# Another order of maps and projection units in the second mixer of a two-block transformer kernel

## What is computed

```python
def token_mixer(h, w_in, w_out, lq1, lk1, lq2, lk2, subln_gain, rel_bias, layer):
    proj = h @ w_in
    ...
    oa = diff_attention(qa, ka, va, lam, rel_bias[:, :2 * N_DIFF_HEADS])
    oa = rmsnorm(oa, subln_gain) * (1.0 - lam0)
    ...
    ob = dilated_attention(qb, kb, vb, rel_bias[:, 2 * N_DIFF_HEADS:])
    ...
    mixed = jnp.concatenate([oa, ob], axis=-1)
    return mixed @ w_out
```

## Time and profile before

| | before |
|---|---|
| runs | 1048.93, 1046.16, 1045.85 us |
| the profiled execution's own time | 1050.62 us |
| its span | 1048.5 us |
| PE busy | 1006.0 us (96%) |
| DVE, ACT, POOL busy | 666.6, 477.8, 80.7 us |
| moved by DMA | 175.77 MB, 168 GB/s over the span |

### The profile page before, as it was taken

How to read it: one execution, slowest core, us unless ns; L and a number is a source line. 1 busy time by engine, 2 the same in 40 slices (tenths; PEclk the granted TensorE clock), 3 DMA queues, 4 the chain that set the end, 5 groups by cost and what they waited for, 6 DMA issues and landing times. The chain is left out here.

```text
span 1048.5 us, 17492 instructions
## 1 busy us (share of the span) xinstructions
PE 1006.0 (96%) x7506; PEld 958.7 (91%) x7506; DVE 666.6 (64%) x848; ACT 477.8 (46%) x573; POOL 80.7 (8%) x202
## 2 busy tenths in 40 slices
PE   4999998999999999999999999999997899999996
PEld 4999998989999999999899999989997899999995
DVE  3578865685876866666675555556667366555554
ACT  4455555554435544444543434444434254434343
POOL 0010104532140000000000000000002000000001
PEclk9999999999999999999999999999999699999999
DMA  8656545342456555464556565654333146565641
GB/s 280 203 162 190 179 155 162 125 157 96 146 165 223 189 189 202 166 209 166 182 170 199 179 199 178 200 163 161 121 121 121 47 162 215 164 201 177 197 146 40
DMA packets 143558, 175.77 MB, mean 168 GB/s; under 512 B 4661, under 2 KB 130777, under 8 KB 143482
## 3 DMA queue, kind: packets, MB, share of 16 engines
q1 hardware_dynamic: 138794, 168.30, 49.4%
q10 hardware_dynamic: 4688, 6.36, 1.9%
HBM read 173.58 MB, written 4.22 MB: 170 GB/s over the span
## 5 line engine op out<-in xcount | busy, mean ns | idle before, releaser
L336 PE MATMUL ps<-hTh,wh 128*128 128x256 f32 x1512 | 431.3, 285 | 7.5 <-DVE wl L1227 6.9
L1227 DVE TENSOR_TENSOR wl<-raw,wh 128x2048 fp32r<-128x2048 f32 (+1 forms) x156 | 356.6, 2287 | 115.2 <-ACT wh L841 114.9
L336 PE MATMUL ps<-hTl,wh 128*128 128x256 f32 x1512 | 428.2, 283 | 0.0
L336 PE MATMUL ps<-hTh,wl 128*128 128x256 f32 x1512 | 428.1, 283 | 0.0
L841 ACT ACTIVATE wh<-raw 128x2048 fp32r<-128x2048 f32 (+1 forms) x158 | 299.5, 1900 | 177.9 <-PE ps L336 177.4
L336 PEld LDWEIGHTS ps<-hTh,wh 128*128 128x128 f32 x1512 | 289.7, 192 | 11.1 <-DVE wl L1227 6.7
L336 PEld LDWEIGHTS ps<-hTl,wh 128*128 128x128 f32 x1512 | 289.7, 192 | 1.4
L336 PEld LDWEIGHTS ps<-hTh,wl 128*128 128x128 f32 x1512 | 289.6, 192 | 0.2
L336 PE MATMUL ps<-wh,yTh 128*128 128x512 f32 (+1 forms) x328 | 123.9, 378 | 1.4 <-DVE BIGT L1625 1.3
L336 PE MATMUL ps<-wl,yTh 128*128 128x512 f32 (+1 forms) x328 | 124.5, 380 | 0.0
L336 PE MATMUL ps<-wh,yTl 128*128 128x512 f32 (+1 forms) x328 | 122.6, 374 | 0.0
(11 more groups left out here) (253 smaller groups left out, 811.6 us busy)
## 6 DMA issues: line engine op xcount, KB each, us to landing
raw<-in_ffn_w_up SPq DMA_DIRECT2D x44, 1024.0 KB, 5.3
raw<-in_w_in SPq DMA_DIRECT2D x40, 1024.0 KB, 5.3
raw<-in_ffn_w_down SPq DMA_DIRECT2D x33, 1024.0 KB, 5.1
raw<-in_ffn_w_gate SPq DMA_DIRECT2D x22, 1024.0 KB, 5.3
raw<-in_w_out SPq DMA_DIRECT2D x8, 1024.0 KB, 5.0
raw<-in_mem_kv_w SPq DMA_DIRECT2D x4, 1024.0 KB, 5.0
scr_f<-scr_r ACTq DMA_DIRECT2D x1, 3072.0 KB, 15.3
raw<-in_w_br_hgrn SPq DMA_DIRECT2D x2, 1024.0 KB, 5.0
```

The source lines that it names most:

```text
L336: ins = pe.matmul(o, l(k), r(k), start=first and k == ks[0] and j == 0, stop=last and k == ks[-1] and j == 2)
L1227: dve.tensor_tensor(wl[j % NS][:, 0:n], raw[j % NR][:, 0:n], wh[j % NS][:, 0:n].bitcast(F32), ALU.subtract).then_inc(w_lo, 1)
```

## The change

Seven things are altered, all between these two points.

- The maps are in another order: the eight diff maps first, then the eight dil maps. The weights are in the order qa0, ka0, va0, qa1, ka1, va1, qb0, kb0, qb1, kb1, vb0, vb1.
- `rows_out` and `toks_out` take a function `mid` that is called between their halves, so PE's map steps stand one at each half unit, where two stood at the end of a unit.
- Six buffers hold turned maps, PT0, PT1 and four in `Hn` (idle in this stage), so a dil map's values may come up to six maps after its turns. The values of maps 8 to 15 are issued in groups of two and three, behind vb's units.
- `scores` of map 8 and 12 also wait for qb; `diff_out` waits for the head before it.
- ACT and DVE have their work in a new order, with `exps` 14 and 15 and the drain of vb1 behind the split of OA.
- The output projection's first two units run side by side in four banks: the k blocks 0 to 3 of both (OA), then 4 and 5 (OB's first half), then 6 and 7, with the last steps of the maps and the two turns of OB between them.
- `project`'s stretches for the first block are tuples in place of functions, with the same waits.

```diff
+        PT2 = PT + [Hn[:, 512 * j:512 * j + 512] for j in range(4)]
...
+        def turned(a, i):
+            return PT[i % 2] if a == 0 else PT2[i % 6]
...
-            def rows_out(key, banks):
+            def rows_out(key, banks, mid=None):
...
+                    if m == 0 and mid:
+                        mid()
...
+            def step(s=None, t=None, vs=()):
+                if s is not None:
+                    scores(1, s)
+                if t is not None:
+                    turns(1, t)
+                for v in vs:
+                    values(1, v)
+
             toks_out(("va", 0), W)
...
+            step(0)
+            rows_out(("qa", 1), W, mid=lambda: step(1, 0))
+            step(2, 1, [0])
+            rows_out(("ka", 1), W, mid=lambda: step(3, 2, [1]))
+            step(None, 3, [2])
+            toks_out(("va", 1), W, mid=lambda: step(4, None, [3]))
+            step(5, 4)
+            rows_out(("qb", 0), W, mid=lambda: step(6, 5, [4]))
+            step(7, 6, [5])
+            rows_out(("kb", 0), W, mid=lambda: step(None, 7, [6]))
+            step(None, None, [7])
+            rows_out(("qb", 1), W, mid=lambda: step(8))
+            step(9, 8)
+            rows_out(("kb", 1), W, mid=lambda: step(10, 9))
+            step(11, 10)
+            toks_out(("vb", 0), W, mid=lambda: step(12, 11))
+            step(13, 12)
             pe.wait_ge(oa_done, 1)
             for p in range(2):
                 turn(("oa", p), OA, p, 512)
...
+            toks_out(("vb", 1), W, mid=lambda: step(14, 13, [8, 9]))
+            step(15, 14, [10, 11])
...
+            ts_a = begin_unit(key_a, W)
+            pe.wait_ge(*free(("oa", 0)))
+            pe.wait_ge(*free(("oa", 1)))
+            stretch(key_a, ts_a, (0, 1, 2, 3))
+            step(None, 15, [12, 13, 14])
+            ts_b = begin_unit(key_b, T)
+            stretch(key_b, ts_b, (0, 1, 2, 3))
+            pe.wait_ge(*free(("bo", 0)))
+            turn(("ob", 0), OB, 0, 512)
+            step(None, None, [15])
+            pe.wait_ge(*free(("ob", 0)))
+            stretch(key_a, ts_a, (4, 5))
+            pe.wait_ge(*free(("bo", 1)))
+            turn(("ob", 1), OB, 1, 512)
+            stretch(key_b, ts_b, (4, 5))
+            pe.wait_ge(*free(("ob", 1)))
+            stretch(key_a, ts_a, (6, 7))
+            stretch(key_b, ts_b, (6, 7))
+            toks_out(("wo", 4, PIECES[2]), W, yhT_at)
```

More of the change, by code:

```diff
@@ L25 @@
 MAPS1 = [("fox", h) for h in range(8)] + [("mem", h) for h in range(4)]
-MAPS2 = ([("diff", h, j) for h in (0, 1) for j in (0, 1)] + [("dil", h) for h in range(4)]
-         + [("diff", h, j) for h in (2, 3) for j in (0, 1)] + [("dil", h) for h in range(4, 8)])
-OBANK = {("diff", 0): 6, ("diff", 1): 7, ("dil", 0): 6, ("diff", 2): 7, ("diff", 3): 6, ("dil", 1): 7}
+MAPS2 = [("diff", h, j) for h in range(4) for j in (0, 1)] + [("dil", h) for h in range(8)]
+OBANK = {("diff", 0): 6, ("diff", 1): 7, ("diff", 2): 6, ("diff", 3): 7, ("dil", 0): 6, ("dil", 1): 7}
 class Banks:
@@ L613, in attend @@
             def attend(a, i):
[L614 to L618, removed]
+                if 0 <= i - 1 < 12:
                     turns(a, i - 1)
-                if 0 <= i - 2 < n:
+                if 0 <= i - 2 < 12:
                     values(a, i - 2)
-                if not early and i < n:
+                if i < 12:
                     scores(a, i)
@@ L709, in project @@
                         weights(i)
-                        for ks, before in stretches:
-                            before()
+                        for ks, operands_made in stretches:
+                            pe.wait_ge(*operands_made)
                             for m in range(2):
@@ L1607, in attend @@
             def attend(a, i):
-                n = 12 if a == 0 else 16
-                early = a == 1 and i != 12
-                if early and i < n:
-                    guards(a, i)
-                if 0 <= i - 1 < n:
+                if 0 <= i - 1 < 12:
                     copies(a, i - 1)
-                if 0 <= i - 2 < n:
+                if 0 <= i - 2 < 12:
                     outs(a, i - 2)
-                if not early and i < n:
+                if i < 12:
                     guards(a, i)
@@ L1708, in project @@
                     begin(key)
[L1709 to L1713 removed]
+                    if n == 0 or (k, n) == (4, 1):
                         for m in range(2):
@@ L1831, in dve_program @@
                 turn_lo_part(("oa", p), yTh, yTl, p, gs)
-            attend(1, 16)
+            guards(1, 14)
+            copies(1, 13)
+            begin(("vb", 1))
+            guards(1, 15)
+            copies(1, 14)
+            outs(1, 11)
+            copies(1, 15)
+            turn_lo_part(("ob", 0), hTh, hTl, 0)
+            outs(1, 15)
+            turn_lo_part(("ob", 1), hTh, hTl, 1)
             project(4)
```

194 lines of the change are left out of this document (89 added, 105 removed).

## The result

| | before | after |
|---|---|---|
| median of the runs | 1046.16 us (3 runs, known when the prediction was made) | 1034.20 us (4 runs, 1034.12 to 1034.22) |
| the kernel before, run beside it | 1047.55 us (4 runs, 1045.85 to 1049.07) | |
| ratio after / before | | 0.9873 [0.9853, 0.9893] |
| the profiled execution's own time, its span | 1050.62, 1048.5 us | 1034.2, 1032.1 us |
| PE, DVE, ACT, POOL busy | 1006.0, 666.6, 477.8, 80.7 us | 997.5, 666.4, 478.3, 80.6 us |

The kernel is 1.3% faster. Against the base of the prediction, 1046.16, that is 12.0 us. DVE, ACT and POOL do the same work. PE's busy time fell by 8.5 us although it has the same matmuls; a matmul that runs at the low clock counts as busy for longer.

A forecast was written before the change was run, and what follows sets the result against it. PE was taken to bound the kernel, 104.0 us of the 122.1 us stretch being work. New waits and seams made 107.0, 15.1 less; 1046.2 - 15.1 = 1031.1 us, range 1028.0 to 1037.

The forecast's parts named there:

- likeliest case: Whole kernel: the forecast as summed, 1031.1 us, own range 1028.5 to 1033, chance 0.66.
- the clock rival: Stretch: clock falls all the same, or unprofiled runs never had so much to win; 1033.6 to 1037 us, chance 0.18.
- 18.1 us of waits and clock: va0 to first turn behind third output unit: 122.1 us less 104.0 of work; about 12 waits, some 6 clock.
- Map steps, slack 1.9 us: Steps at half units: 4.57 us from scores to turns where 2.69 are needed; pairs' waits, 2.0 us, go.
- The knot at 794: PE's waits for bank, copy and exponentials near 794 us, some 3.5 us, go with six buffers and later dil values.
- OA's norm covered by 1.5 us: OA scaled on POOL at 791.4 us, turned by PE at 792.9, so the old 2.2 us wait goes.
- The rival of the other order: At OA's norm DVE's weight split takes the port before POOL's product: PE waits 1.4 us, 1032.2 us total, chance 0.10.
- Entry wait 1.4: Entry into the output projection: PE waits 1.4 us for ACT's drain of vb1, now behind the last map's exponentials.
- OB 1.1 and 0.2: OB's turns: 1.1 us of wait stay open at the first half, 0.2 at the second; old 1.7 and 0.8 go.
- No fall of the clock: Stretch: new waits of 1.4 and 1.1 us, some 10 us apart, bring no low clock; 6 us come back.
- New stretch 107.0: va0 to first turn behind third output unit: 104.0 + 1.4 + 1.1 + 0.2 + 0.3 us against 122.1.
- The slower one: All 16 maps' steps late, PE pausing throughout with the clock low: 1055 us, chance 0.02.

The follow-up runs named there:

- both waits taken away: Changed kernel with vb1's drain ahead of the last map's exponentials and OB's first half turned before the second output unit's first matmuls: 1032.61 us, 0.9854 of before.
- the kernel with six operations: Changed kernel with six small POOL operations added, each waiting for the last, ahead of POOL's scaling of OA: 1038.36 us.
- the drain's move: Changed kernel with vb1's drain on ACT ahead of the last map's exponentials instead of behind them: 1033.80 us, 0.9866 of before.
- the serial kernel: Changed kernel with its first two output units one after the other again and both halves of OB turned together: 1038.45 us, 0.9900 of before.
- the 2.3 us of the rest: Changed kernel with half-unit steps and side-by-side output units both undone, leaving orders and six buffers: 1046.27 us, 0.9978 of before.

## Why the prediction was right, and which step was not

1031.1 us were forecast, 1034.20 measured: 3.1 us more. That is outside the likeliest case's own range (to 1033) and inside the whole one (1028 to 1037). It lies in the range of the clock rival, 1033.6 to 1037, which gave two ways to get there: the clock falls all the same, which did not happen, or the unprofiled runs never had so much low clock to win back, which did. The account of the stretch was right; that the time came out inside the range rests on the room that this rival had made.

- **What bounds the kernel, and 18.1 us of waits and clock: right in kind.** With both waits taken away the stretch is pure work and takes 103.09 us. The prediction built 104.0 from a unit of 5.84 us; the chains show 5.74 to 5.78 (72 matmuls in 8.61 us; halves of 2.86 and 2.92). Thirteen units make up about 1 us of it.
- **Map steps, slack 1.9 us, cost nothing: right.** 4.50 us instead of 4.57, no wait on exponentials. Undoing it costs 9.8 us of stretch, more than the 2.0 us of the old pairs' waits: 6.8 are waits on exponentials, because seven maps' turns would again come too soon behind their scores, 0.9 a longer entry wait and 1.5 the clock. The sum did not need that number, but its attribution, 2.0 us to the placement and 3.5 to the knot, treated the parts as separate; the runs show they are not.
- **The knot at 794 goes: right**, no wait there, but the reading of it was not. The prediction has PE waiting "for bank and copy" and gives the credit to the six buffers. The row names DVE's scaling of the k unit (HG, L1311) as the releaser: before, only the turns of map 11 and the values of map 10 stood between kb1 and the scores of map 12. In the new order step 11 and half of vb0 stand between them. With the old order and the steps at half units the wait was 2.12 us, and with the new order but neither half units nor side-by-side units there is none, so it is the order that takes it away; buffers were part of both new-order kernels and were not tested apart.
- **OA's norm covered by 1.5 us: right**, 1.35. POOL's product was first, DVE's split took 3.71 us instead of 2.28 (1.4 longer; 1.3 forecast). The rival of the other order did not occur in the two profiles of this kernel; the kernel with six operations shows a short POOL operation held in this way, not the product. By the Trainium skill (SBUF — State Buffer, "Who interferes with whom") the earlier instruction keeps the shared ports to its end; 789.31 against 789.65 and 789.70 against 789.40 agree with it in both directions.
- **Entry wait 1.4: right, 1.21**, and its cause shown by the drain's move. **OB 1.1 and 0.2: 1.0 and 0.** **Seams 0.3:** nothing to be seen; the work came out below its estimate with them in it.
- **No fall of the clock: right.** The argument by the size of the waits held as far as it was tried: behind 1.05 and 0.85 us no profile has the clock down, behind 2.3 us it was. But size alone does not decide. The same wait of 2.0 us at 233 us was followed by a fall in three profiled executions of fourteen, and 0.89 and 1.73 us within 3 us were followed by one in the serial kernel, while 1.85 and 1.2 us at 794 in the earlier trace rows were not. A forecast of "no fall" behind waits of such a size is a chance, not a certainty.
- **New stretch 107.0: measured 105.45.** The forecast for the profiled execution, 1035.5, was 1.3 us too high, mostly the units' work and the seams.
- **The step that failed is the last of the sum:** "it is 4.5 us above the median, and against that median 1046.2 - 15.1". The 4.5 us of excess were taken off the forecast as if both kernels had them. It was low clock inside the very stretch that the change clears: a run at a mean clock of 0.990 had some 16 us to gain, one at 0.996 only 12 (1046.27 - 1034.20 = 12.1 between two profiles, of which 117.08 - 105.45 = 11.6 in the stretch). And the three runs that made the base had two from the quick end of a kernel whose median over 61 runs is 1048.41. Against that median the change brings 14.2 us, near the 15.1; against 1046.16, 12.0. The prediction held the right sentence, in a rival: "if the profile's 4.5 us above the median are clock alone, the gain shrinks to 10.6". The premise was true. The figure came out at 12.0 and not 10.6 because the execution gained 16.4 us where 15.1 were summed, and it should have been the main line: the new time does not depend on what clock the old one had. The two errors partly cancel: 4.5 us too low by the excess, 1.3 us too high by the stretch, 3.1 us too low in all. The plain sum, 1035.5 for a profile without any low clock in the stretch, was closer to the median (1.3 us off) than the corrected one.

**The rivals.** The clock's fall did not come: all eight runs of the changed kernel have a mean of 0.997 or 0.998. Its second condition, little low clock to win back, was met. Late steps: none of the 16. No net change: no. The slower one, 1055 us by pauses all along, did not come; the nearest thing is the old order with steps at half units, 1050.51 us, where it was not small pauses at each map but four large ones near the end of the stretch.

**Left open.** The six buffers were not taken away by themselves, so how the 2.3 us of the rest divide between order and buffers is not known. Why an unchanged kernel's clock comes back after one fall in some executions and goes on falling in others is not told by any run here, nor why it fell behind the same 2.0 us wait in three executions of fourteen. Of the unprofiled runs only the mean clock is known, not where it was low.

## What to carry to other kernels

When a profiled execution is slower than the median and its excess is low clock inside the stretch that a change clears, build the new time up from the new stretch's work and waits; do not subtract the excess from both. Compare stretches, not only whole times: about 1 us of the difference in three runs here lay in code that no edit touched. In this kernel, spreading steps on the bounding engine paid only where the places that it then reached earlier (a drain, a norm) had also been moved; else the waits gathered at the last of them, and in one heap they cost the clock as well. After such a change, look for what is left by the kind "issue" too: here two moved calls, one of them found that way, gave another 1.6 us.

## What the runs showed of the hardware that was not expected

- One kernel, one order of work: 1045.9 to 1051.7 us in 61 runs, in step with the mean granted clock (0.996 to 0.990). In the two of them that were profiled the waits agree, and the difference is whether TensorE, once at the low level (0.50, which is 1.2 GHz) near 813 us, is back at 2.4 GHz by 818 or is still at 0.50 between 818 and 822 and again between 828 and 832, behind the wait for OB.
- The same wait of 2.0 us at the same place of the same code was followed by the low clock in 3 of 14 profiled executions (0.72 between 234 and 240 us) and not in the other 11 (1.00); where it came it cost 1.5 us (489.8 instead of 488.3 us from there to va0).
- In this kernel a single wait of 2.3 us on an otherwise busy TensorE was followed by the low clock (means of 0.87 between 793 and 796 and 0.56 between 796 and 799), which cost 1.6 us of stretch beyond the wait. Behind 3.6 us of waiting it cost 1.5 and behind 7.0 us 1.9, so the price hardly grew with the wait.
- In each of the three kernels with a chain of added GpSimd operations on 128x8 numbers, one was held for 2.1 to 2.4 us by a DVE weight split begun up to 0.3 us before it, while a GpSimd product begun 0.34 us before a split cost that split 1.4 us.
